# A two-block model of 512 tokens on one core: 352 instead of 384 tokens go through the expert tables, 160 instead of 128 are gathered, and splits, copies and waits of other stages move between engines

## What is computed

```
p   = modulate(rmsnorm(x, norm1), sh1, sc1) @ w_in         # SSD gate z, conv channels, dt, Hyena channels
ssd: depthwise conv, silu, softplus(dt); chunked scan: cumsum(dt * A), states per chunk,
     decay products C.B^T * exp(segsum) and C.state * exp(cumsum); gated norm
hyena: filters = mlp(positions) * exp(-t * deltas); two long convolutions through DFT matrices
h   = x + g1 * (concat(ssd, hyena) @ w_out)
f   = modulate(rmsnorm(h, norm2), sh2, sc2)
def peer(f):                                               # 8 heads, 128 x 128 keys, 16384 experts
    s1, i1 = top_k(q1 . subkeys1, 16); s2, i2 = top_k(q2 . subkeys2, 16)
    sc, ci = top_k(s1[:, None] + s2[None, :], 16)          # 128 choices a token
    idx = i1[ci // 16] * 128 + i2[ci % 16]; gate = softmax(sc)
    act = gelu(einsum('td,thkd->thk', f, u_tab[idx])) * gate
    return einsum('thk,thkd->td', act, v_tab[idx])
h   = rmsnorm(h + g2 * peer(f), final_norm)
```

## Time and profile before

| | |
|---|---|
| median of 3 runs | 4386.53 us (4385.96 to 4389.57) |
| the profiled execution's own time | 4381.67 us |
| its span, first to last instruction | 4379.9 us |
| mean granted TensorE clock | 0.975 |
| PE busy | 4206.7 us (96%) |
| DVE busy | 2993.5 us (68%) |
| ACT busy | 1805.0 us (41%) |
| POOL busy | 1425.4 us (33%) |
| moved by DMA | 665.76 MB, mean 152 GB/s |

### The profile page before, as it was taken

How to read it: one execution, slowest core, us unless ns; L and a number is a source line. 1 busy time by engine, 2 the same in 40 slices (tenths; PEclk the granted TensorE clock), 3 DMA queues, 4 the chain that set the end, 5 groups by cost and what they waited for, 6 DMA issues and landing times.

```text
span 4379.9 us, 66702 instructions
## 1 busy us (share of the span) xinstructions
PE 4206.7 (96%) x26175; PEld 3683.5 (84%) x26175; DVE 2993.5 (68%) x5043; ACT 1805.0 (41%) x2815; POOL 1425.4 (33%) x992
## 2 busy tenths in 40 slices
PE   7989999999999999999999999999999999999998
PEld 5756755779999999999999877799889877877997
DVE  5866667559768977777688455498388445555873
ACT  4345411233335643333355345355255333324542
POOL 2044224315886545766411210212111110112121
PEclk9989999999999999999999999899999999899999
DMA  5123521224887899999733222123323332002332
GB/s 188 63 92 127 185 69 58 90 90 149 281 267 283 332 369 364 368 373 373 263 97 106 92 79 72 61 92 97 99 92 101 101 104 92 26 36 68 107 97 77
DMA packets 232191, 665.76 MB, mean 152 GB/s; under 512 B 22519, under 2 KB 88455, under 8 KB 229704
## 3 DMA queue, kind: packets, MB, share of 16 engines
q1 hardware_dynamic: 110528, 389.87, 26.6%
q0 software_dynamic: 38752, 142.91, 8.9%
q10 hardware_dynamic: 82600, 128.71, 8.3%
HBM read 593.25 MB, written 68.16 MB: 151 GB/s over the span
## 4 chain that ended last, share of the span: by engine, by line
PE 81%; DVE 10%; issue 3%; ACT 3%; POOL 2%; DMA 1%; ACTq 0%; DVEq 0%; POOLq 0%
PE ps L273 15%; PE ps L275 15%; PE ps L274 15%; PE ps L2743 5%; PE ps L2745 5%; PE ps L2744 5%; PE ps L1624 2%; PE ps L2337 2%; PE ps L3778 1%; PE ps L1703 1%; DVE A L912 1%; DVE r L292 1%; DVE r L242 1%; DMA A<-in_w_late 1%; PE ps L405 1%
## 5 line engine op out<-in xcount | busy, mean ns | idle before, releaser
L273 PE MATMUL ps<-r,r 128*128 128x384 f32 (+1 forms) x3944 | 1435.8, 364 | 14.8 <-POOL r L242 7.2
L274 PE MATMUL ps<-r,r 128*128 128x384 f32 (+1 forms) x3944 | 1418.8, 360 | 0.0
L275 PE MATMUL ps<-r,r 128*128 128x384 f32 (+1 forms) x3944 | 1418.3, 360 | 0.0
L236 ACT ACTIVATE r<-A 128x1024 fp32r<-128x1024 f32 x513 | 542.0, 1058 | 1132.7 <-PE ps L275 996.8
L242 DVE TENSOR_TENSOR r<-A,r 128x1024 fp32r<-128x1024 f32 x401 | 509.0, 1271 | 728.2 <-ACT r L236 715.9
L273 PEld LDWEIGHTS ps<-r,r 128*128 128x128 f32 x3944 | 743.0, 188 | 101.0 <-issue 13.6
L274 PEld LDWEIGHTS ps<-r,r 128*128 128x128 f32 x3944 | 743.0, 188 | 74.6 <-issue 3.6
L275 PEld LDWEIGHTS ps<-r,r 128*128 128x128 f32 x3944 | 742.2, 188 | 74.1
L289 ACT ACTIVATE r<-A 128x512 fp32r<-128x512 f32 (+1 forms) x796 | 474.1, 611 | 497.9 <-DVE A L2429 227.9
L2743 PE MATMUL ps<-r,r 128*128 128x256 f32 x2128 | 603.0, 283 | 3.4 <-DVE A L2907 2.6
L2744 PE MATMUL ps<-r,r 128*128 128x256 f32 x2128 | 602.2, 283 | 0.0
...
## 6 DMA issues: line engine op xcount, KB each, us to landing
A<-in_pu SPq DMA_DIRECT2D x128, 512.0 KB
A<-in_pv SPq DMA_DIRECT2D x128, 512.0 KB
...
acts<-A ACTq DMA_DIRECT2D x128, 192.0 KB
...
```

The lines of the kernel that those rows point to most:

```text
L236: a.activation(self.vr(self.wr0 + 2048 * (u % RW), 1024), self.v(self.st0 + 1024 * (u % RS), 1024), ACT.Copy).then_inc(*self.S.on("a", "hi ...
L273: t.matmul(o, hi, xh, start=first and k == k0, stop=False)
L274: t.matmul(o, hi, xl, start=False, stop=False)
L275: m = t.matmul(o, lo, xh, start=False, stop=final and k == K - 1)
```

## The change

The constant NT goes from 384 to 352, and 160 tokens' worth of rows are gathered: the rows 0 to 127 as before for tokens 0 to 127, and 32 more gathers of u and of v for tokens 128 to 159, four choices at a time on the four groups of 32 partitions (`x again` makes four copies of those tokens, `moved` their indices). There are 88 gate steps, written out 2816 KB and read back 704 KB at a time; an activation tile is 176 KB; the rows are spread over finer steps. The activations of the last 14 u tiles stay in SBUF (`act_at`). In every second one-hot matrix GpSimd does the multiplication by the gate. GpSimd also makes the low parts of units wq 8 to 15 and u 0 to 2.

Besides: the sums ahead of tile 14 go into banks 2 and 3 and no longer wait for `tok 10`; the modulation's fifth row has a bank of its own; ScalarE copies the filter tiles out of PSUM and GpSimd multiplies two of eight; two units' low parts move behind the norm's `rstd`; with K = 8 `back_t` runs the whole group and then warms and sums; and the four units at the head of the decay products go into their loop.

```diff
-UT, NT, LATER = 76, 384, 14
+UT, NT, LATER = 76, 352, 14
+NG, TG = 512 - NT, NT // 8
...
-        self.lo_of = ["g" if wq + RW < u <= wq + 128 - LATER or u == 16 else "v" for u in range(len(self.units))]
+        self.lo_of = ["g" if wq + RW - 11 < u <= wq + 128 - LATER or u == 16 else "v" for u in range(len(self.units))]
...
         v.reciprocal(r, var).then_inc(*S.on("v", "rstd", tag))
+        self.weights_v(v, units)
...
                 t.wait_ge(*S.at("aa"))
-                t.wait_ge(*S.at("tok", 10))
...
                         at = 32 * c + 16 * d
-                        m = t.matmul(PS[4][:, at:at + 16], self.cst(tri), self.v(L.AA + at, 16), start=True, stop=True)
...
             for k in range(3 * n, 3 * n + 3) if n < 8 else ():
-                if k in (8, 16):
-                    t.wait_ge(*S.at("modrow", 3 + k // 8))
-                self.modmm_t(t, 4 + k // 8, 6, range(k % 8, k % 8 + 1))
+                if k == 16:
+                    t.wait_ge(*S.at("modrow", 4))
...
         self.after(a, "a", "states")
-        self.weights_a(a, 32)
         a.activation(self.stat(4)[:, 0:1], self.cst("one1"), ACT.Exp).then_inc(*S.on("a"))
...
+            if o in (2, 3, 4, 5):
+                self.weights_a(a, 8)
...
-        self.weights_v(v, 32)
         self.modset_v(v, 6, 4)
...
+            if o in (3, 4, 5, 6):
+                self.weights_v(v, 8)
...
+    def filters_a(self, a, r):
+        S = self.S
+        if r:
+            a.wait_ge(*S.at("ks", r - 1, 1, 3))
+        for i in range(8):
+            if self.filter_direct(r, i):
+                continue
+            a.wait_ge(*S.at("fil", r, i))
+            a.activation(self.filter_out(i)[0], self.ps("fil", r, i)[:, :], ACT.Copy).then_inc(*S.on("a", "out", "fil", r, i))
...
+    def filters_g(self, g, r):
+        S = self.S
+        g.wait_ge(*S.at("filter decay", r))
+        for i in self.FILTER_G:
+            h, dec = self.filter_out(i)
+            g.wait_ge(*S.at("out", "fil", r, i))
+            g.tensor_tensor(h, h, dec, ALU.mult).then_inc(*S.on("g"))
+        S.mark("g", "filter half", r)
...
-        self.weights_v(v, 16)
...
-        for at, m in ([(("choices", i), 16 * (i + 1) // 3) for i in range(9)] + [(("gates", i), 48 + 55 * (i + 1) // 96) for i in range(96)]
-                      + [(("later", r), 103 + r + 1) for r in range(LATER)]
-                      + [(("second", x), min(117 + x + 1, 128) if x < 11 else 128 + min(128, 128 * (x - 10) // 108)) for x in range(128)]):
+        for at, m in ([(("choices", i), 64 * (i + 1) // 27) for i in range(27)] + [(("gates", i), 64 + 76 * (i + 1) // (NT // 4)) for i in range(NT // 4)]
+                      + [(("later", r), 140 + 17 * (r + 1) // LATER) for r in range(LATER)]
+                      + [(("second", x), min(157 + x + 1, NG) if x < 5 else NG + min(NG, NG * (x - 4) // 117)) for x in range(128)]):
...
+        if n == 128:
+            g.wait_ge(*S.at("moved"))
...
+    def act_at(self, c):
+        L = self.L3
+        if c < 128 - LATER or c >= 124:
+            return L.SP + NT * (c % 4)
+        i = c - 128 + LATER
+        return L.KEPT + NT * i if i < 7 else self.HX + 2816 + NT * (i - 7)
...
-    ROWS = {14 + 17 * n // 16: n for n in range(48)}
+    ROWS = {c: [n for n in range(64) if 14 + 7 * n // 8 == c] for c in range(UT)}
...
                 m.then_inc(*S.on("t", "x tokens", i))
+                ps = self.bank_t(t, "x again", i)
+                for q in range(4):
+                    x = self.v(L.SC0 + 512 * (4 * i + q) + 128, NG - 128)
+                    for c in range(4):
+                        m = t.matmul(ps[32 * c:32 * c + 32, 128 * q:128 * q + 128], x, self.cst("ident"), start=True, stop=True)
...
+        if rows is not None:
+            self.rows_v(v, "choices", rows)
...
+        if rows is not None:
+            self.rows_v(v, "choices", rows + 1)
...
             v.tensor_tensor(h, io, e2, ALU.is_equal).then_inc(*S.on("v", "one hot", b))
+            if b % 2 == 0:
+                v.tensor_tensor(a, io, e1.unsqueeze(2).to_broadcast([128, 8, 128]), ALU.is_equal).then_inc(*S.on("v", "one hot 1", b))
+                return
             for q in range(8):
                 v.tensor_scalar(a[:, q, :], self.PS[2][:, 0:128], e1[:, q:q + 1], gate[:, q:q + 1], ALU.is_equal, ALU.mult).then_inc(*(S.on("v", "one hot gated", b) if q == 7 else S.on("v")))
+
+    def hot_g(self, g, b):
+        S = self.S
+        if b < NT // 8 and b % 2 == 0:
+            a, h, e1, e2, gate = self.one_hot(b)
+            g.wait_ge(*S.at("one hot 1", b))
...
+        self.hot_g(g, 0)
+        for n in range(64, 68):
             self.gather(g, n)
         for i in range(NT // 4):
+            if i % 2 == 0:
+                self.hot_g(g, i // 2 + 2)
             if self.gates_early(i) is not None:
...
-    FIRST = 6
+    FIRST = 5
...
-        if 0 <= slot - 3 < 128:
-            self.act_load(a, slot - 3)
+        if slot % 4 == 3 and slot // 4 + 1 < 32:
+            self.gate_load(a, slot // 4 + 1)
...
+        tag, k0 = ("ln", i), K - 8
         for o in range(start, 8):
...
-        self.norm_seven_t(t, tag, wk, self.LN, True)
-        self.group(t, [ps[:, :]], [rhs], K, "back", i, 7, k0=k0, first=False)
-        self.warm_t(t, 0 if i in (1, 4) else 2, 1)
+        if k0:
+            self.group(t, [ps[:, :]], [rhs], k0, "back", i, 7, "first part", final=False)
+            self.norm_seven_t(t, tag, wk, self.LN, True)
+            self.group(t, [ps[:, :]], [rhs], K, "back", i, 7, k0=k0, first=False)
+            self.warm_t(t, 0 if i in (1, 4) else 2, 1)
+        else:
+            self.group(t, [ps[:, :]], [rhs], K, "back", i, 7)
+            self.warm_t(t, 0 if i in (1, 4) else 2, 4)
+            self.norm_seven_t(t, tag, wk, self.LN, True)
         self.norm_last_t(t, tag, ("res", i, 7), wk, self.LN, True)
```

More of the change, by code:

```diff
@@ L442, in off_four_v, with norm_apply_v @@
             v.scalar_tensor_tensor(out=self.H(k), in0=self.PS[b][:, :], scalar=-1.0 / 512, in1=self.H(k), op0=ALU.mult, op1=ALU.add).then_inc(*S.on("v", "off four", tag, k))
-    def norm_apply_v(self, v, tag, last, dsts, gains, eps, banks, mean, parts):
+    def norm_apply_v(self, v, tag, last, dsts, gains, eps, banks, mean, parts, units=0):
         S = self.S
@@ L1546, in load_filter @@
             a.wait_ge(*S.at("filter", r - 1))
+            a.wait_ge(*S.at("filter half", r - 1))
         for i, x in enumerate((L.a, L.b)):
@@ L1614, in spectrum_t @@
             t.wait_ge(*S.at("filter", r))
+            t.wait_ge(*S.at("filter half", r))
         else:
@@ L1823, in long_s @@
         s.wait_ge(*S.at("filter", 3))
+        s.wait_ge(*S.at("filter half", 3))
         s.wait_ge(*S.at("scan kept"))
@@ L1983, in long_g @@
             self.product_g(g, r, 0)
+            if r < 3:
+                self.filters_g(g, r + 1)
             self.product_g(g, r, 1)
@@ L2000, in lay_peer @@
         L.XT, L.ROWS, L.ACC = self.al(1024), self.al(6144), self.al(1024)
-        L.DOT, L.COEF, L.GATE, L.IDX = (self.al(128) for _ in range(4))
+        L.DOT, L.COEF, L.GATE, L.IDX = (self.al(NG) for _ in range(4))
         L.SP = self.al(4 * NT)
@@ L2075, in rows_a @@
         S, L = self.S, self.L3
-        if L.steps[at] and L.steps[at][-1] == 127:
-            a.wait_ge(*S.at("row used", 127))
-            a.activation(self.v(L.COEF, 128), self.v(L.DOT, 128), ACT.Gelu).then_inc(*S.on("a", "row acts"))
+        if L.steps[at] and NG - 1 in L.steps[at]:
+            a.wait_ge(*S.at("row used", NG - 1))
+            a.activation(self.v(L.COEF, NG), self.v(L.DOT, NG), ACT.Gelu).then_inc(*S.on("a", "row acts"))
     def topk_s(self, s):
@@ L2218, in best_v @@
             v.max(v8(i, 1), part(alt, i)).then_inc(*S.on("v", "max 2", what, tt, i))
+        if rows is not None:
+            self.rows_v(v, "choices", rows + 2)
         for i in range(n):
@@ L2242, in topk_v @@
             v.wait_ge(*S.at("x tokens", i))
-            v.wait_ge(*S.at("out", "x tokens", i))
         v.wait_ge(*S.at("residual kept", "peer"))
@@ L2300, in topk_g @@
             self.weights_g(g, 8)
-            if c in self.ROWS:
-                if self.ROWS[c] == 0:
+            for n in self.ROWS[c]:
+                if n == 0:
                     g.wait_ge(*S.at("chosen"))
-                    g.wait_ge(*S.at("out", "x tokens", 1))
-                self.gather(g, self.ROWS[c])
+                    g.wait_ge(*S.at("out", "x again", 1))
+                self.gather(g, n)
     def gates_early(self, i):
```

167 lines of the change are left out of this document (103 added, 64 removed).

## The result

The changed kernel takes **4347.84 us** (median of 3 runs, 4345.2 to 4351.8), against 4386.53 before: ratio 0.9918, 95% interval 0.9894 to 0.9942. It is faster, by 39 us where 75 were forecast (4311). The time lies 2 us inside the range's upper end, and the gain is half of what the sum said. The profiled execution has a span of 4346.0 us, 33.9 less than before.

A forecast was written before the change was run, and what follows sets the result against it. The prediction took TensorE and DMA to be both about full in the experts. Its terms summed to -75 us on the profiled 4381.7, giving 4306.7, and 4311 for the median; range 4270 to 4350.

The forecast's parts named there:

- Hyena: Hyena's long convolutions: ScalarE's copying of filter tiles removes TensorE's waits for filters and banks, -13 us (-5 to -18).
- 76 u tiles: Experts' first u tiles: GpSimd becomes the pace, 4.12 us for 56 tiles, waits for used rows go; -17 us.
- Gate steps and last u tiles: Experts' gate steps at 233 us, VectorE the pace, then last 14 u tiles at 55 us; together -12 us.
- v tiles: Experts' v tiles: 4.10 us each limited by transfers, TensorE the pace from about x = 103; -14 us.
- The sums: First block's front: sums ahead of tile 14 no longer wait for VectorE to free their bank, -6 us.
- States: First block's states and modulation: waits at bank changes go, partly met by weights' transfers, -5 us.
- Decay products: First block: head starts 5 us earlier without its units, which cost 1 us inside the loop; -4 us.
- Rival 5: Front and Hyena: waits only move, 20 of the 36.5 us gain are lost, 4331 us; chance 10%.
- Rival 1: Experts: transfers keep up and TensorE is the pace in all four windows, 4254 us; chance 10%.
- Rival 2: Experts: 370 GB/s is the transfers' ceiling, so the experts give nothing, 4359 us; chance 17%.
- Rival 3: Gate steps: handing one-hot matrices from VectorE to GpSimd stalls, 0.5 us more a pair, 4333 us; chance 15%.
- Rival 4: U tiles: GpSimd's multiplication and VectorE's two-operand work hold each other up, kernel slower, from 4396 us; chance 3%.

The follow-up runs named there:

- second profile: The changed kernel, unedited, profiled again in a later run: 4344.06 us, ratio 0.9920 to the kernel before.
- e1: Changed kernel with VectorE multiplying all eight Hyena filter tiles straight from PSUM, none copied or given to GpSimd: 4341.34 us, ratio 0.9908 to the kernel before.
- e5: Changed kernel with ScalarE copying only the two filter tiles GpSimd multiplies, VectorE taking six from PSUM: 4335.74 us, ratio 0.9902 to the kernel before.
- e9: Separate small kernel timing VectorE instructions alone and beside GpSimd's additions: both operands in SBUF 0.704 us alone, 1.678 beside; one in PSUM 0.682 beside.
- e4: Changed kernel with GpSimd making half of each u tile's low part and, from the 17th, half of each activation's: 4327.29 us, ratio 0.9886 to the kernel before.
- e11: Changed kernel with the modulation's own bank undone, all three rows in one PSUM bank: 4353.68 us, ratio 0.9946 to the kernel before.
- e14: Changed kernel gathering only 128 rows of v a token group instead of 160: 4313.67 us, ratio 0.9860 to the kernel before.
- e8: Changed kernel with VectorE making the whole first one-hot pair, other even pairs keeping GpSimd's multiplication: 4337.60 us, ratio 0.9902 to the kernel before.

## Why the prediction was wrong, and where it was right

The direction was right; the gain was not, and the time is inside the range by 2 us only, so that is as much luck as foresight. The sum is off by 41 us: 24 in Hyena, 11 in the 76 u tiles, 6 in gate steps and last u tiles, 6 in the v tiles; all other stages together came out 6 better than forecast.

- **Hyena, the step that failed** ("VectorE still multiplies six of eight, but is 1.3 us a round shorter"): the step priced a filter at 0.68 us from a copy too. It takes 1.24 on average, because both operands are now in SBUF while GpSimd works; the 1x512 sums beside it (L1639) went from 0.68 to 1.39. -13 became +11 (+8 in the second profile), 21 to 24 us of the 41 in the two profiles. e1 and e5 show that the copies cost 9 to 14 us of Hyena, e9 why. The rest is the wait for filter tiles that was to be gained; no run gained it (it is back in e5).
- **76 u tiles** (-17): the mechanism was right, GpSimd as the pace (e4); the waits for rows did go. The size was off: 4.28 us a tile against 4.12 (56 x 0.16 = 9 us), since GpSimd also waits for high parts (8.7 us in 240), and TensorE 5.6 us for the first pair, which no term held. -6 measured.
- **Gate steps and last u tiles** (-12): the steps came out at 228.3 against 233. VectorE, which the sum made the pace, is busy 206 of 228 us and waits 24 for rows, so the nearness of the two numbers is in part luck; GpSimd's multiplication takes 1.90 us instead of 2.4. The last u tiles lost 5.3 us where 6 were to be gained: with half rows they take 51.5 us instead of 60.2, with half of VectorE's or GpSimd's work 60.3 and 60.9, so it is the transfers, which I had put at 3.9 us a tile. -6 measured.
- **v tiles** (-14): 4.10 us forecast, 4.09 and 4.04 measured for tiles 8 to 104, at 389 and 396 GB/s from 1700 to 2000 us, inside the bounds of 4.00 to 4.15. That TensorE takes over from x = 103 was wrong: 16 tiles from there take 64 to 67 us, not 61.4. -8 and -16 in the two profiles. The Trainium skill (DMA: Bandwidth & Descriptors, section Specifications) gives 358 GB/s as one core's half of a stack's 716; the one core that runs here reads faster than that, so that figure is no limit for this kernel.
- **The sums** (-6): -5.7, but 1.9 come back: the first state now waits 5.1 us for the convolution's last tile on ScalarE. **States** (-5): -11.4, of which 8.6 are the bank (e11) where the waits of 6.0 stood in the rows; what gives the other 2.8 is not told apart (the granted clock is 0.87 before, 0.89 in e11). **Decay products** (-4): the head's gain was right (12.1 to 6.9 us), its price in the chain was set at 1 and is 3.6.
- **Norms**: -1.6 for 1.5 ahead of the experts. From the start of GpSimd's four additions to the turns of the result, norm 1 took 24.3 us and takes 17.2, 7.1 less for 5.5; norm 4 took 19.3 and takes 17.9, 1.4 for 1.5. The rest of the second block varies by more than that between executions.
- **Copies and folding** (+4.5): +2.7 for the copies; the folding is not told apart.

Of the four large terms of the forecast's own case only the v tiles came out near their sum. Rival 5 (waits in front and in Hyena only move, 4331) is true of Hyena and did not go far enough; the front gave back less than it gained. Rival 1 (transfers keep up) did not come true; with 9% fewer bytes and fewer row instructions (e14) TensorE is the pace. Rival 2 gave the number nearest to the measured one (4359), but its mechanism was refuted by 389 to 396 GB/s. Rival 3 (GpSimd's one-hot matrices stall the gate steps) was small: TensorE waits 5.6 us for the first and 5.5 us for four others, and taking the first back to VectorE gains nothing (e8). Rival 4 had the mechanism that failed Hyena, GpSimd and VectorE's two-operand work holding each other up, but placed it in the u tiles, where GpSimd's low part went from 2.55 to 2.47 us; the forecast never asked for it in Hyena.
